# Halved norms on one core: VectorE makes the modulated block, and PSUM banks are named at four boundaries

## The reference, cut to what matters

```
x = x + gate * y                       (residual)
r = rsqrt(mean(x*x) + eps)             (per token)
h = (x * r * g) * (1 + scale) + shift  (modulated block, input of the next products)
```

## Time and profile before

| what | value |
|---|---|
| three runs, median | 2740.75 us (2738.27 to 2741.63) |
| the profiled execution | 2740.4 us, span 2738.6 us |
| mean granted TensorE clock | 0.993 |
| PE busy | 2668.8 us (97% of the span) |
| PEld busy | 2148.9 us (78%) |
| DVE busy | 1391.9 us (51%) |
| ACT busy | 1034.7 us (38%) |
| POOL busy | 110.1 us (4%) |
| chain that ended last | PE 90%, ACT 2%, DVE 2% |

### The profile page before, as it was taken

The page is one execution under the profiler, slowest core; times in us unless marked ns, Lnnn a source line. Parts: engine busy times, 40 slices in busy tenths (PEclk is TensorE's granted clock), DMA queues, the critical chain, the costliest instruction groups (busy, mean ns, idle before and its releaser), DMA issues.

```text
span 2738.6 us, 32934 instructions
## 1 busy us (share of the span) xinstructions
PE 2668.8 (97%) x13810; PEld 2148.9 (78%) x13810; DVE 1391.9 (51%) x2147; ACT 1034.7 (38%) x1525; POOL 110.1 (4%) x87
## 2 busy tenths in 40 slices
PE   7989999999999999999999999999999999999998
PEld 3578888877777777888888777788888777788887
DVE  6767767544444445543445654543444554543343
ACT  2243233453333334532343554422233555432232
POOL 0000000000000000000000110010010110010010
PEclk9989999999999999999999999999999999999999
DMA  7445645322222121223223121223223121223232
GB/s 299 185 161 207 247 180 204 116 82 78 78 78 72 68 78 62 78 98 110 93 94 121 50 81 55 101 94 105 92 97 118 62 77 62 92 93 115 78 104 74
DMA packets 46850, 297.03 MB, mean 108 GB/s; under 512 B 5104, under 2 KB 7280, under 8 KB 17520
## 3 DMA queue, kind: packets, MB, share of 16 engines
q1 hardware_dynamic: 46560, 294.42, 29.5%
q10 hardware_dynamic: 144, 0.52, 0.1%
HBM read 292.82 MB, written 2.10 MB: 108 GB/s over the span
## 4 chain that ended last, share of the span: by engine, by line
PE 90%; ACT 2%; DVE 2%; issue 0%; DVEq 0%
PE PS L506 88%; PE PS L564 1%; DVE WL L1414 1%; ACT H1H L972 0%; ACT WH L972 0%; DVE AR L1437 0%; DVE XT L1417 0%; DVE AA L1414 0%; ACT H2Hb L972 0%; ACT V0b L972 0%; ACT V1b L972 0%; DVE H1L L1414 0%; ACT AA L972 0%; ACT V2b L972 0%; ACT OC L972 0%
## 5 line engine op out<-in xcount | busy, mean ns | idle before, releaser
L506 PE MATMUL PS<-H1H,WH 128*128 128x512 f32 (+1 forms) x2256 | 885.8, 393 | 20.3 <-DVE WL L1414 12.6
L506 PE MATMUL PS<-H1H,WL 128*128 128x512 f32 (+1 forms) x2256 | 865.5, 384 | 0.0
L506 PE MATMUL PS<-H1L,WH 128*128 128x512 f32 (+1 forms) x2256 | 864.8, 383 | 0.0
L1414 DVE TENSOR_TENSOR WL<-RAW,WH 128x1024 fp32r<-128x1024 f32 (+1 forms) x400 | 526.8, 1318 | 461.3 <-ACT WH L972 460.7
L972 ACT ACTIVATE WH<-RAW 128x1024 fp32r<-128x1024 f32 (+1 forms) x400 | 439.7, 1101 | 270.0 <-PE PS L506 242.8
L506 PEld LDWEIGHTS PS<-H1H,WH 128*128 128x128 f32 x2256 | 427.6, 190 | 114.0 <-DVE WL L1414 16.7
L506 PEld LDWEIGHTS PS<-H1L,WH 128*128 128x128 f32 x2256 | 427.8, 190 | 84.3 <-issue 5.5
L506 PEld LDWEIGHTS PS<-H1H,WL 128*128 128x128 f32 x2256 | 427.1, 189 | 83.0
L506 PE MATMUL PS<-H2Hb,WH 128*128 128x512 f32 (+1 forms) x408 | 162.5, 398 | 4.0 <-issue 3.0
L506 PE MATMUL PS<-H2Hb,WL 128*128 128x512 f32 (+1 forms) x408 | 155.1, 380 | 0.0
L506 PE MATMUL PS<-H2Lb,WH 128*128 128x512 f32 (+1 forms) x408 | 154.8, 380 | 0.0
(11 more groups left out here) (252 smaller groups left out, 3085.0 us busy)
## 6 DMA issues: line engine op xcount, KB each, us to landing
RAW<-stream SPq DMA_DIRECT2D x170, 1024.0 KB, 4.8
AR<-stream SPq DMA_DIRECT2D x56, 1024.0 KB, 6.9
RAW<-stream SPq DMA_DIRECT2D x64, 704.0 KB, 4.0
RT<-ret SPq DMA_DIRECT2D x2, 1536.0 KB, 6.8
MIX<-stream SPq DMA_DIRECT2D x4, 640.0 KB, 14.1
XT<-xt SPq DMA_DIRECT2D x2, 1024.0 KB, 8.8
y<-XT SPq DMA_DIRECT2D x16, 128.0 KB, 1.8
COND<-c ACTq DMA_DIRECT2D x1, 512.0 KB, 5.0
```

Source lines behind the costliest of these rows:

```text
L506: return nc.tensor.matmul(out, weights, moving, start=start, stop=stop, skip_group_check=True)
L1414: return nc.vector.tensor_tensor(out, a, b, op)
```

## The change

Five edits go together.

- `banks()` takes for each boundary a list of eight banks, for the halves, the norm and the three entry tiles. After it the rotation goes on with the same count n as before.
- `entry`: TensorE does chunks 0 to 3 of tile t0, then chunks 0 to 3 of tile t0 + 1, then the norm matmul of part 1, then chunks 4 to 7 of both side by side. After that it is as before.
- The float32 copy V is made by VectorE from T with a `tensor_scalar` (multiply by gain, add shift) for the 16 units at norm1, norm2 and norm3. ACT makes only the high part of them. DVE's order is a staircase: step n issues `divide(n)`, `shift(n - 1)`, `low(n - 2)`, with the residual of chunk 6, part 1 after step 1, `half_sum` and `prep(t0 + 1)` after step 2, the residual of chunk 7, part 1 after step 4, and `prep(t0 + 2)` after step 5. ACT's order is changed to match.
- At norm2 the queries' V (still made by ACT) goes to six buffers of its own, and the wait for all 16 key/value lows is gone.
- At the end ACT multiplies x by `final_g_2` ahead of time, in place; DVE's last pass is a `tensor_tensor` by the root alone.

```diff
-    def halves(t, v):
-        for key in ((t, 0), (t + 1, 0), (t, 1), v, (t + 1, 1)):
-            take(key)
+    def halves(t, v, among):
+        for key, b in zip(((t, 0), (t + 1, 0), (t, 1), v, (t + 1, 1), *range(t + 2, min(t + 5, NTILE))), among):
+            take(key, (b,))
...
-    halves(15, "norm1")
-    for t in range(FFN0, ATT0 - 2):
+    halves(15, "norm1", (0, 1, 2, 3, 4, 5, 6, 0))
+    for t in range(FFN0 + 3, ATT0 - 2):
         take(t)
-    halves(ATT0 - 2, "norm2")
-    for t in range(ATT0, ATT0 + 3):
-        take(t, (2, 3, 4))
+    halves(ATT0 - 2, "norm2", (5, 6, 0, 7, 1, 2, 3, 4))
...
-    halves(FFN1 - 2, "norm3")
-    for t in range(FFN1, IN0):
+    halves(FFN1 - 2, "norm3", (0, 1, 4, 7, 2, 3, 5, 6))
+    for t in range(FFN1 + 3, IN0):
         take(t)
...
-    halves(NTILE - 2, "last")
+    halves(NTILE - 2, "last", (0, 1, 2, 3, 4))
@@ entry
-        for k in range(8):
-            if k == 4:
-                half_norm(v, bank, 1)
+        for x in range(2):
+            for k in range(4):
+                some(x, 0, k)
+        half_norm(v, bank, 1)
+        for k in range(4, 8):
             for x in range(2):
                 some(x, 0, k)
@@ act_program
-            act(part_of(c.H1H, k, part), T, ACT.Identity, **kw)
-            q.wait_ge(c.nld, n + e - 3 if e > 3 else n)
-            act(c.NORM[v]["V"][e % 4][:, 0:256], T, ACT.Identity, **kw).then_inc(c.nv, 1)
+            act(part_of(c.H1H, k, part), c.NORM[v]["T"][e % 3][:, 0:256], ACT.Identity,
+                scale=c.AB[:, gains + k:gains + k + 1], bias=c.mod(shift + k, 1)).then_inc(c.nh, 1)
@@ act_program, edge
         half_root(v, bank, out, 0)
+        make(0, 0)
+        make(0, 1)
         half_square(v, 6, 1, first)
+        make(0, 2)
         prep(t0 + 1)
-        for k in range(4):
-            make(0, k)
+        make(0, 3)
+        make(0, 4)
         half_square(v, 7, 1, first)
         prep(t0 + 2)
-        make(0, 4)
         make(0, 5)
+        make(0, 6)
         half_root(v, bank, out, 1)
-        make(0, 6)
         make(0, 7)
@@ act_program, queries at norm2
-        q.wait_ge(c.al1, 16)
-        q.wait_ge(c.al0, k - 2)
-        act(c.AV[k % 3][:, :], chunk(c.AT, k), ACT.Identity, **kw).then_inc(c.av0, 1)
+        q.wait_ge(c.al0, k - 5)
+        act(c.AV0[k % 6][:, :], chunk(c.AT, k), ACT.Identity, **kw).then_inc(c.av0, 1)
@@ dve_program, edge
+        for n in range(18):
+            if n < 16:
+                divide(n)
+            if 1 <= n < 17:
+                shift(n - 1)
+            if n >= 2:
+                low(n - 2)
+            if n == 1:
+                left(6, 1)
+            elif n == 2:
+                half_sum(v, 1)
+                prep(t0 + 1)
+            elif n == 4:
+                left(7, 1)
+            elif n == 5:
+                prep(t0 + 2)
...
+            nc.vector.tensor_scalar(c.NORM[v]["V"][e % 4][:, 0:256], c.NORM[v]["T"][e % 3][:, 0:256],
+                                    c.AB[:, gains + k:gains + k + 1], c.mod(shift + k, 1), ALU.mult, ALU.add
+                                    ).then_inc(c.nv, 1)
@@ dve_program, last pass
-            stt(x, x, c.cols("final_g_2", k), part_of(c.SG, 0, part), ALU.mult, ALU.mult).then_inc(c.yd, 1)
+            q.wait_ge(c.gained, k + 1 + 2 * part if k >= 6 else k + 1)
+            tt(x, x, part_of(c.SG, 0, part), ALU.mult).then_inc(c.yd, 1)
```

More of the change, by code:

```diff
@@ L327, in __init__ @@
         self.AT = at("Tb", 206336, 4096)
-        self.AV = [at(f"V{i}b", 222720 + 2048 * i, 512) for i in range(3)]
+        self.AV = at("Vb", 222720, 1024)
+        self.AV0 = [at(f"V{i}b", 148480 + 2048 * i, 512) for i in range(6)]
         self.SB = [at("SB0", 203840, 1024), at("SB1", 209984, 1024)]
@@ L399, in __init__ @@
             sem(n) for n in ("ya", "yc", "sa", "si", "sp", "gm", "gh", "gl"))
-        self.at, self.av1, self.av0, self.al0, self.al1 = (sem(n) for n in ("at", "av1", "av0", "al0", "al1"))
+        self.at, self.av1, self.ah1, self.av0, self.al0, self.al1 = (
+            sem(n) for n in ("at", "av1", "ah1", "av0", "al0", "al1"))
         self.qk, self.vf, self.vt, self.vv, self.s1, self.b4, self.ex, self.nd = (
@@ L418, in __init__ @@
             sem(n) for n in ("fmm", "fln", "frs", "fy", "fg", "fh", "fl"))
-        self.yd = sem("yd")
+        self.gained, self.yd = sem("gained"), sem("yd")
     def xk(self, k):
@@ L1140, in ffn @@
                     square(v, n, True)
+                if f == 3:
+                    act(c.xk(n), c.xk(n), scale=c.cols("final_g_2", n)).then_inc(c.gained, 1)
                 if gains is not None:
@@ L1144, in act_program @@
     q.wait_ge(c.gain, 5)
-    edge(1, BANK["norm1"], RES["pool"], FFN0, c.NORM[1]["R"], modulated(1, 1, 8, 24))
+    edge(1, BANK["norm1"], RES["pool"], FFN0, c.NORM[1]["R"], high(1, 1, 8, 24))
     table("silu")
@@ L1150, in for_kv @@
     def for_kv(part, k):
[L1152 to L1158, removed]
+        q.wait_ge(c.at, 8 * part + k + 1)
+        act(part_of(c.AH, k, part), part_of(c.AT, k, part), ACT.Identity, scale=c.AB[:, 24 + k:25 + k],
+            bias=c.mod(96 + k, 1)).then_inc(c.ah1, 1)
     q.wait_ge(c.gain, 7)
@@ L1255, in act_program @@
         square(3, n)
-    edge(3, BANK["norm3"], RES[WO0], FFN1, c.NORM[3]["R"], modulated(2, 3, 32, 72))
+    edge(3, BANK["norm3"], RES[WO0], FFN1, c.NORM[3]["R"], high(2, 3, 32, 72))
     table("silu")
@@ L1396, in act_program @@
     last = RES[FFN3] + 8
[L1397 to L1404, removed]
+    for part in range(2):
+        for k in (6, 7):
+            half_square(8, k, part, last)
+        if part == 0:
+            q.wait_ge(c.gl, 88)
+            q.wait_ge(c.sp, 44)
+        half_root(8, BANK["last"], c.SG, part)
+        for k in (6, 7):
+            x = part_of(c.XT, k, part)
+            q.wait_ge(c.sq, SQN[8] + k + 1 + 2 * part)
+            act(x, x, scale=c.cols("final_g_2", k)).then_inc(c.gained, 1)
 def dve_program(c):
@@ L1474, in over_rms, with edge @@
         tt(c.NORM[0]["T"][k % 3][:, :], c.xk(k), c.NORM[0]["R"][:, :], ALU.mult).then_inc(c.nt, 1)
-    def edge(v, first, t, gate, t0, divide, low):
+    def edge(v, first, t, gate, t0, divide, shift, low):
         def left(k, part):
@@ L1526, in over_root, with make @@
     def over_root(a, v, first):
-        def make(part, k):
-            e, n = 8 * part + k, 16 * a - 16
+        def make(e):
+            part, k = divmod(e, 8)
+            n = 16 * a - 16
             q.wait_ge(c.nrs, NORMN[v] + 1 + part)
             q.wait_ge(c.res, first + 8 + 2 * part)
+            q.wait_ge(c.nh, 8 + n + e - 2 if e > 2 else 8 + n)
             q.wait_ge(c.nv, n + e - 2 if e > 2 else n)
@@ L1535, in over_root, with shifted, make @@
         return make
-    def low_half(a, v):
-        def make(part, k):
-            e = 8 * part + k
-            q.wait_ge(c.nv, 16 * a - 16 + e + 1)
+    def shifted(a, v, gains, shift):
+        def make(e):
+            k, n = e % 8, 16 * a - 16
+            q.wait_ge(c.nt, 8 + n + e + 1)
+            q.wait_ge(c.nld, n + e - 3 if e > 3 else n)
+            nc.vector.tensor_scalar(c.NORM[v]["V"][e % 4][:, 0:256], c.NORM[v]["T"][e % 3][:, 0:256],
+                                    c.AB[:, gains + k:gains + k + 1], c.mod(shift + k, 1), ALU.mult, ALU.add
+                                    ).then_inc(c.nv, 1)
+        return make
+    def low_half(a, v):
+        def make(e):
+            part, k = divmod(e, 8)
+            n = 16 * a - 16
+            q.wait_ge(c.nv, n + e + 1)
+            q.wait_ge(c.nh, 8 + n + e + 1)
             tt(part_of(c.H1L, k, part), c.NORM[v]["V"][e % 4][:, 0:256], part_of(c.H1H, k, part).bitcast(F32),
@@ L1658, in dve_program @@
     gains(5, 8, "norm2_g", 0, 32)
-    edge(1, RES["pool"], 15, 16, FFN0, over_root(1, 1, RES["pool"]), low_half(1, 1))
+    edge(1, RES["pool"], 15, 16, FFN0, over_root(1, 1, RES["pool"]), shifted(1, 1, 8, 24), low_half(1, 1))
     ffn(0, FFN0, 2, 40)
@@ L1663, in dve_program, with kv_root @@
     gains(8, 32, "norm2_g", 8, 80)
-    def attention_root(part, k):
+    def kv_root(e):
+        part, k = divmod(e, 8)
         q.wait_ge(c.nrs, NORMN[2] + 1 + part)
@@ L1669, in attention_root, with kv_shifted, kv_low @@
         tt(part_of(c.AT, k, part), part_of(c.XT, k, part), part_of(c.SG, 0, part), ALU.mult).then_inc(c.at, 1)
-    def kv_low(part, k):
-        e = 8 * part + k
+    def kv_shifted(e):
+        part, k = divmod(e, 8)
+        q.wait_ge(c.at, e + 1)
+        q.wait_ge(c.al1, e - 3)
+        nc.vector.tensor_scalar(c.AV[:, 256 * (e % 4):256 * (e % 4) + 256], part_of(c.AT, k, part), c.AB[:, 24 + k:25 + k],
+                                c.mod(96 + k, 1), ALU.mult, ALU.add).then_inc(c.av1, 1)
+    def kv_low(e):
+        part, k = divmod(e, 8)
         q.wait_ge(c.av1, e + 1)
-        tt(part_of(c.AL, k, part), c.AV[e % 3][:, 0:256], part_of(c.AH, k, part).bitcast(F32), ALU.subtract
-           ).then_inc(c.al1, 1)
```

(9 more changed lines are left out.)

6 lines of the change are left out of this document (2 added, 4 removed).

## The result

The changed kernel takes 2754.16 us (median of four runs, 2753.64 to 2757.30) beside 2740.14 us for the kernel before: slower, ratio 1.0054, 95% interval [1.0036, 1.0071]. Forecast were 2752.9 us within 2747 to 2757.5. The profiled execution is the longest of the four, 2757.3 us with a span of 2755.5, against 2740.4 and 2738.6 before.

A forecast was written before the change was run, and what follows sets the result against it. Behind the entries of norm1 and norm3, unbroken TensorE work was taken as the bound. Losses of 18.2 us less gains of 5.8 give 12.4 us on 2740.4, written as 2752.9 us; range 2747 to 2757.5.

The forecast's parts named there:

- Edit 4, the stops: New bank lists at norm1 and norm3: TensorE waits 7.2 us at tile 20 and 5.4 us at tile 160.
- Rival B: At tiles 20 and 160 the bank waits do not bind; only the gains are left, 2735.0 us; chance 0.09.
- The slow clock behind the stops: Behind tile 20's and tile 160's stops: granted clock 0.50 for about 6 us, 2.8 us lost each time.
- Rival C: Both stops come, but TensorE leaves them at or near full clock, 5.6 us less, 2747.3 us; chance 0.10.
- Edit 2, norm2: At norm2, TensorE's 2.96 us wait before the entry goes and tile 81's transposes come earlier; gain 3.4 us.
- stays as it is: Behind tile 81's transposes at norm2: 3.7 us of TensorE idle time remains ahead, so the slow clock there is unchanged.
- Edit 3, the end: Last pass at 0.34 instead of 0.41 us spacing; last residual, root and second pass move earlier; gain 0.5 us.
- Edit 1, the entries: V on VectorE in staircase steps of 0.95 us; norm1's entry gains 1.2 us, norm3's 0.7 us.
- drain rule: At the entries' VectorE steps: next operation starts only after the pipe empties, a 1.20 us step; left out of the sum.
- the same steps without modulation work: At norm3 the staircase runs as at norm1; unit 7 ends 0.85 us earlier, with 0.7 us counted.
- Rival D: Both stops, and the staircase slower than ACT's pace; norm1, norm3 and half of norm2 give nothing, 2756.7 us; chance 0.09.
- the risk: At norm1 TensorE's 1.8 us wait before unit 4 may drop the clock, losing 0.7 of the 1.4 us gain.

The follow-up runs named there:

- turns kept: The changed kernel with the banks at norm1 and norm3 put back to the old turns, norm2's new list kept; 2738.29 and 2737.20 us on two chips.
- norm3 collides: turns kept with norm3's bank list as in the changed kernel, so only norm3's banks collide; 2746.28 us, ratio 1.0014.
- experiment 7: The changed kernel with its colliding bank lists left in and only TensorE's entry order put back to chunk by chunk; 2752.11 us, ratio 1.0044.
- experiment 3: The kernel before with the changed kernel's bank lists and nothing else; 2757.26 us, ratio 1.0058.
- experiment 2: The run of norm3 collides: only norm1's banks put back in the changed kernel; 2746.28 us, ratio 1.0014.
- experiments 3 and 4: The kernel before with all changed bank lists, 2757.26 us; and the kernel before with only norm2's banks changed, 2740.26 us.
- (1): The run of turns kept: the changed kernel with norm1's and norm3's banks in the old turns; 2738.29 us, ratio 0.9988.
- experiment 6: turns kept with TensorE's entry matmuls back in the old order, compared with turns kept; 2734.82 us, ratio 0.9979.
- chunk by chunk: turns kept with TensorE's old entry order, both tiles side by side, norm matmul ahead of chunk 4; 2734.82 us, again 2734.19 us.

## Why the prediction was right

**Edit 4, the stops.** Right in place, releaser and size: 7.13 and 5.33 us against 7.2 and 5.4, shown by taking the collisions away (turns kept), by putting one back (norm3 collides) and by having them alone in the kernel before. What made the sizes exact was to see that the chain to the first product by up 0 hangs on the entry's end; experiment 7 tested that directly. Rival B (the bank is free in time) is out.

**The slow clock behind the stops.** Right that it comes, and a little less in the profiled execution: 2.42 and 1.68 us for twice 2.8, from the earlier trace rows. The granted clock was already 0.65 within the first stop and still 1.00 in the second, and behind them 0.57 and 0.73 over 6 us. The same two stretches lost 2.7 and 1.9 us in experiment 3, 1.5 and 2.5 in experiment 7, and the second 2.9 in experiment 2, so 2.8 was near the top of what comes. By ratios or medians the two stops cost 17.0 us (experiments 3 and 4), 17.9 (7) and 18 (1), of which 12.5 are waits: 4.5 to 5.6 for the clock against 5.6 forecast, with the uncertainty of two medians on each. Rival C (full clock behind the stops) is out. The page that speaks against it, the Trainium skill, "TensorE: Matmul & The Clock Gate", section "What's actually happening", has the lower level as the default which activity has to lift; both stops agree with it, the second only in part.

**Edit 2, norm2.** Forecast a gain of 3.4 us ahead of the transposes; 3.1 came. Norm2's bank alone gives 1.6 of it, V on VectorE the rest (34.03 and 34.04 us with V on ScalarE and the new bank, 32.14 to 32.57 with V on VectorE in all executions but turns kept, which the last section tells of). The sentence that the slow clock behind the transposes "stays as it is" did not hold: 1.15 us more came there, and as shown above most of it was luck. TensorE's wait at the transposes is 3.74 us, as forecast (3.7):

```profile
574.73 0.58 ACT L974 ACTIVATE VF<-PS 128x512 f32<-128x512 f32 x1
```

```profile
575.36 0.66 PE L564 MATMUL PS<-BAS,VF 128*128 128x128 f32 x4 [3.74 <-ACT VF L974]
```

**Edit 3, the end.** Forecast 0.5, measured 0.52. The pass is 2.77 us long for eight, 0.34 a spacing:

```profile
2744.26 2.77 DVE L1415 TENSOR_TENSOR XT<-XT,SG 128x256 f32<-128x256 f32 x8
```

**Edit 1, the entries: the step that failed.** The tensor_scalar was taken at 0.27 us between starts and takes 0.32, a step of 0.99 for 0.95; that is 0.3 us over eight steps. The Trainium skill's drain rule ("VectorE: DVE Perf Modes", "The DRAIN you can't avoid") was left out rightly: an operation of 0.41 us lets the next start after 0.32. The same section adds that a next operation which is not held starts earlier, and that is the case that the traces show. The larger miss is the sentence on norm3, "the same steps without modulation work". I had worked out at norm1 when the second root comes and found it just in time. There the modulation work holds DVE in the middle of the entry and gives TensorE time. At norm3 nothing holds DVE, and the root comes when TensorE, in its new order, has got through its waits: DVE waited 2.67 us for it, and the entry became 1.83 us longer where 0.7 shorter was forecast:

```profile
1129.34 0.47 ACT L974 ACTIVATE Rc<-PS,KON 128x256 f32<-128x256 f32 x1 [2.73 <-PE PS L506]
```

```profile
1130.30 0.43 DVE L1415 TENSOR_TENSOR T2c<-XT,Rc 128x256 f32<-128x256 f32 x1 [2.67 <-ACT Rc L974]
```

About 0.8 of this goes with the clock, which was at its lower level in that entry for twice as long as in that of turns kept (25.67 against 24.89 us; the row of turns kept stands at experiment 6, and before the entry ran at 1.00):

```profile
1122.80:1129.60 6.80, 6.37 (x25) 0.50 0.28 118
```

The rest is the order, as chunk by chunk shows (22.9 to 23.1). Rival D (the staircase slower than ACT's pace) is out by that as well: with the same tensor_scalar and the old order the entries of norm2 and norm3 are shorter than with V on ScalarE, by 1.9 and 0.7 us or more, and that of norm1 is not longer (32.1 to 32.5 against 32.6). At norm1 0.63 of 1.2 us arrived. The clock fell behind the short waits there, which the prediction had named as the risk, and with it the second root came too late here too:

```profile
165.50:167.90 2.40, 1.25 (x7) 0.81 0.87 307
167.90:173.40 5.50, 5.50 (x22) 0.50 0.57 238
```

```profile
174.15 0.43 DVE L1415 TENSOR_TENSOR T2a<-XT,Ra 128x256 f32<-128x256 f32 x1 [0.79 <-ACT Ra L974]
```

In turns kept DVE did not wait there, and the gain was 1.27 us, as forecast.

So the total was right because the large terms were: stops 18.2 against 17.0 to 18, gains 5.8 against 3.3 to 4.2 for turns kept. That it came within 1.3 us (2754.16 for 2752.9) is partly luck. The interval of the measured ratio reaches from 10 to 19 us of loss. In the profiled execution norm3's entry cost 2.5 us more than forecast and norm1's gave 0.6 less, while the clock behind the stops cost 1.5 us less and the clock behind the transposes gave back 1.15 that nobody had forecast.

## What to carry to other kernels

When buffers or banks of a rotation are renamed in one place, write down for each one who has it next and when it is freed, up to the point where the old turns are back: here two short lists in a table cost 17 to 18 us, and the whole rest of the rewrite gave less than a quarter of that. When a stall is found, ask what the start of its releasing chain hangs on; if it is the work ahead of the stall, nothing won there shortens it and nothing is lost either. Moving a matmul behind others to feed a consumer sooner delays whatever else waits for it: follow that second consumer at every boundary, not only at one.

## What was not expected of the hardware

A tensor_scalar's price hangs on how its scalars are given, by 0.06 us for each column at 128x256, and not on the number of operations.

The granted clock can fall or hold behind the same short waits. Turns kept and norm3 collides have the same instructions at norm2 and waited 0.43, 0.37 and 0.77 us in both, to 0.01; the windows of PE there are, for turns kept and then for norm3 collides,

```profile
535.20:539.20 4.00, 3.75 (x17) 0.57 0.24 100
```

```profile
533.50:537.50 4.00, 3.69 (x26) 1.00 0.23 96
```

and the stretch to the transposes took 34.06 and 32.54 us. The same is seen between two executions of chunk by chunk: at the head of the third layer one piece of 124 matmuls in the chain took 30.16 us in the first and 31.78 in the second,

```profile
1517.82 30.16 PE PS L506 x124
```

```profile
1516.71 31.78 PE PS L506 x124
```

as it took 30.16 before and 31.39 in the changed kernel, which is 1.2 of the 1.67 us of the table. What decides it was not found; one profile of a kernel can't give a price of 1.5 us or less to an edit where such waits are near.
